# Neighbourhood operands, bias tables and two modulation groups made inside the pair attention, with the bias tables' masks on VectorE

## What is computed

```
x = first_block(x, c, ctx, c_ctx, norm_gain, w_mod, ...)   # DEPTH = 2 layers
return second_block(x, p_2, ...)

# one layer of the first block, cut
modulation of c by w_mod (six groups), norm, one projection to all operands
att  = global_gqa(q, k, v, k_ctx, v_ctx)       # 8 query heads, 2 key heads of 64, 1280 keys
pool = pool_branch(z, w, s)
near = neighbourhood_attn(q, k, v, k_ctx, v_ctx, rpb, rows)   # 4 heads, bias table by relative place
x = x + gate * (concat(att, pool, near) @ w_out)
```

## Time and profile before

| | us |
|---|---|
| median of 3 runs | 3750.84 |
| lowest and highest | 3748.06, 3755.4 |
| the profiled execution, its own time | 3751.04 |
| its span in the trace | 3749.3 |
| busy PE, DVE, POOL, ACT | 3528.4, 2018.6, 1842.0, 1209.2 |
| layer 0: operand stage starts, step 0's scores start | 388.9, 449.0 |
| layer 1: the same | 1270.8, 1312.3 |

### The profile page before, as it was taken

One profiled execution on the slowest core, in us unless ns is written; L12 is line 12 of the kernel. 1 busy time (PEld: TensorE's weight loads), 2 busy tenths in 40 slices (PEclk: granted clock), 3 DMA queues, 4 the chain that ended last, 5 costly groups with the idle time before them and its releaser, 6 DMA issues. The chain is left out here.

```text
span 3749.3 us, 54629 instructions
## 1 busy us (share of the span) xinstructions
PE 3528.4 (94%) x22582; PEld 2715.0 (72%) x22582; DVE 2018.6 (54%) x2278; ACT 1209.2 (32%) x1716; POOL 1842.0 (49%) x1028
## 2 busy tenths in 40 slices
PE   5999899889899899889999999989899999999998
PEld 5888644568788754568887777876587788878877
DVE  4443577552454467553566734555542888884142
ACT  3234244431223344431123422325401444441020
POOL 1443266544255266543455643304444699974433
PEclk9999899999999999999999999999999999999999
DMA  5112200025111200022221220020033122234212
GB/s 189 35 42 69 75 1 1 27 108 207 57 40 61 58 1 1 27 109 83 94 70 45 86 89 24 4 102 1 27 119 140 52 85 85 85 110 163 64 45 73
DMA packets 101933, 257.99 MB, mean 69 GB/s; under 512 B 29232, under 2 KB 38576, under 8 KB 100800
## 3 DMA queue, kind: packets, MB, share of 16 engines
q1 hardware_dynamic: 83008, 215.42, 16.6%
q10 hardware_dynamic: 18688, 39.20, 3.1%
HBM read 200.02 MB, written 54.56 MB: 68 GB/s over the span
## 5 line engine op out<-in xcount | busy, mean ns | idle before, releaser
L1876 PE MATMUL acc<-h_hi,weights_hi 128*128 128x512 f32 (+1 forms) x928 | 347.5, 374 | 6.6 <-DVE h_lo L2045 4.2
L1877 PE MATMUL acc<-h_lo,weights_hi 128*128 128x512 f32 (+1 forms) x928 | 339.0, 365 | 0.0
L1878 PE MATMUL acc<-h_hi,weights_lo 128*128 128x512 f32 (+1 forms) x928 | 338.7, 365 | 0.0
L1104 DVE TENSOR_REDUCE part_max<-aux 128x1 f32<-128x428 f32 (+5 forms) x468 | 252.9, 582 | 152.5 <-PE aux L945 109.8
L2583 PE MATMUL acc<-h_hi,weights_hi 128*128 128x512 f32 x672 | 271.4, 404 | 0.0
L2585 PE MATMUL acc<-h_hi,weights_lo 128*128 128x512 f32 x672 | 262.9, 391 | 0.0
L2584 PE MATMUL acc<-h_lo,weights_hi 128*128 128x512 f32 x672 | 262.3, 390 | 0.0
L2059 DVE RECIPROCAL arena<-arena 128x512 f32<-128x512 f32 (+1 forms) x48 | 141.8, 2953 | 223.2 <-ACT arena L2022 223.2
L1066 ACT ACTIVATE probs<-acc 128x1024 f32<-128x1024 f32 (+1 forms) x168 | 168.4, 1003 | 239.6 <-PE acc L980 236.8
L991 PE MATMUL acc<-probs,v_tok 128*64 128x512 f32 (+3 forms) x864 | 218.3, 585 | 2.5 <-DVE inverse L1124 2.5
L1876 PEld LDWEIGHTS acc<-h_hi,weights_hi 128*128 128x128 f32 x928 | 175.7, 189 | 41.2 <-issue 9.2
(11 more groups left out here) (524 smaller groups left out, 8976.3 us busy)
## 6 DMA issues: line engine op xcount, KB each, us to landing
weights<-in_w_in SPq DMA_DIRECT2D x44, 512.0 KB, 3.5
arena<-in_w_mod SPq DMA_DIRECT2D x6, 2048.0 KB, 9.3
weights<-in_w_up SPq DMA_DIRECT2D x24, 512.0 KB, 4.3
weights<-in_w_out SPq DMA_DIRECT2D x22, 512.0 KB, 4.9
weight_sums<-feed_forward_spill SPq DMA_DIRECT2D x22, 512.0 KB, 4.6
xT<-in_w_up SPq DMA_DIRECT2D x20, 512.0 KB, 4.1
weights<-in_w_mod SPq DMA_DIRECT2D x4, 2048.0 KB, 21.3
mixer_gates<-arena SPq DMA_DIRECT2D x32, 256.0 KB, 2.0
```

Source lines behind the costliest of these rows:

```text
L1104: nc.vector.tensor_reduce(part_max[:, b % 2, j, hh, i:i + 1], max_tile(m)[:, hh, 0:cw], AX_X, ALU.max, negate=True).then_inc(max_done, 1)
L1876: nc.tensor.matmul(out, w_hi[:, b, k, :], hi[:, k, cols], start=(k == 0), stop=False)
L1877: nc.tensor.matmul(out, w_hi[:, b, k, :], lo[:, k, cols], start=False, stop=False)
L1878: return nc.tensor.matmul(out, w_lo[:, b, k, :], hi[:, k, cols], start=False, stop=(k == KD - 1))
```

## The change

`attention_operands` and its block are gone. A class `AttentionOperands` holds the same work, cut into tasks, and `pair_attention` puts these into its own order, in both layers of the first block:

- Ahead of row 0 (`ahead`): turns 0 to 2, then 12 dense matmuls and the twelve maxima of block 0 with two dense ones ahead of each of the next four; flips 0 to 3 behind maxima 4, 6, 8 and 10, each waiting until ACT has copied the former one's bank to the table in SBUF (`keep_head`, 128x1024); in layer 0 the product of the first gate; row 0. ACT begins with one exponential of a single column (`warm`), then rounds the first key head and the first 512 queries; DVE rounds its halves of both.
- In the steps (`within`): turns 3 to 8 in half-steps 4 to 9, the second key head's rounding on ACT and its rest on DVE, in layer 0 the second gate. Of block 1's maxima, the four that had stood ahead of step 0 in layer 0, and all others, are spread evenly over the steps up to row 1.
- The bias tables: mask, add and copy with rim for each of four heads (`table_step`) on DVE, in half-steps from the fifth on that hold no maximum, `prep` or part of a reciprocal. All their operands are in SBUF. POOL has none of them (`BY_POOL = 0`).
- One slot for the gates' weights in place of two: SP loads the second when the first product is through.
- SP issues all diagonals; POOL clears two of their rows, sets the row of ones, makes the rest of the first key head and the fill.

```diff
@@ -843,10 +843,22 @@
                 at -= 1
             tasks.setdefault(at, []).insert(0, ("max", m))
         at -= 1
-        if first == first_exp[p]:
+        if first == first_exp[p] and (p or not early_in):
             for i in reversed(range(n_prep)):
                 tasks.setdefault(at - (n_prep - i), []).insert(0, ("prep", p, i))
+    if early_in:
+        taken = {at for at in tasks if any(task[0] in ("max", "invert", "prep") for task in tasks[at])}
+        for at, task in AttentionOperands.within(gated, taken):
+            tasks.setdefault(at, []).insert(0, task)
     order = [task for at in sorted(tasks) if at < 0 for task in tasks[at]]
+    if early_in:
+        order, later = AttentionOperands.ahead(gated, order)
+        end = next(at for at in tasks if ("row", 1) in tasks[at])
+        held = later + [task for at in range(end) for task in tasks.get(at, ()) if task[0] == "max"]
+        for at in range(end):
+            tasks[at] = [task for task in tasks.get(at, ()) if task[0] != "max"]
+        for i, task in enumerate(held):
+            tasks[1 + i * (end - 1) // len(held)].append(task)
...
@@ -1003,13 +1040,27 @@
 
                 for at, (kind, j, *i) in enumerate(order):
                     if kind == "max":
-                        if at < n_ahead:
+                        if early and at < n_ahead:
+                            if j < 5:
+                                keep_busy(pg, score_slots[0], first_idle if j == 0 else 2)
+                        elif at < n_ahead:
                             keep_busy(pg, outs[1], first_idle if j == 0 else 2 if pieces[j][0] == 0 else 4)
                         maximum(j)
                     elif kind == "row":
-                        if at < n_ahead:
+                        if early and at < n_ahead:
+                            pe.wait_ge(early.kept_flip, NA_HEADS)
+                            keep_busy(pg, score_slots[0], 5)
+                        elif at < n_ahead:
                             keep_busy(pg, outs[1], 5)
                         row(j)
+                    elif kind == "turn":
+                        early.turn(pe, j)
+                    elif kind == "flip":
+                        early.flip_head(pe, j)
+                    elif kind == "gate_product":
+                        early.gate_product(pe, j)
+                    elif kind == "gate_turn":
+                        early.gates.turn(pe, j)
                     elif kind == "sums":
                         sums(j)
                     elif kind == "scores":
...
@@ -1127,8 +1195,20 @@
                         out = pairs[p].q[:, q0:q0 + qn]
                         nc.vector.tensor_tensor(out, out, inverse[:, 0:qn], ALU.mult).then_inc(divided, 1)
 
+                if early:
+                    early.first_by_vector(dve, pairs[0].q, qs[:, 0], wide)
                 for kind, j, *i in order:
-                    if kind == "prep":
+                    if kind == "first_parts":
+                        early.low_by_vector(dve, pairs[0].q, qs[:, 0], slice(0, wide))
+                    elif kind == "rest_dve":
+                        early.rest_by_vector(dve, pairs[0].q, qs[:, 0], slice(wide, q_cols))
+                    elif kind == "second_rest":
+                        early.second_by_vector(dve)
+                    elif kind == "table":
+                        early.table_step(dve, j, *i)
+                    elif kind == "gate_add":
+                        early.gates.add(dve, j)
+                    elif kind == "prep":
                         if (j, i[0]) == (0, 0):
                             first_copies()
                         if i[0] in ((5, 7) if own_keys else (1, 3)):
...
+class AttentionOperands:
...
+    BY_POOL = 0
+
+    @staticmethod
+    def within(gates, taken):
+
+        found = [(4 + i, ("turn", 3 + i)) for i in range(6)]
+        found += [(2, ("second_keys", 0)), (4, ("second_keys", 1)), (6, ("second_rest", 0))]
+        if gates:
+            found += [(1, ("gate_add", 0)), (1, ("gate_turn", 0)), (2, ("gate_keep", 1)), (2, ("gate_product", 1)), (3, ("gate_add", 1)), (3, ("gate_turn", 1))]
+        steps = [("table", h, i) for h in range(AttentionOperands.BY_POOL, NA_HEADS) for i in range(3)]
+        free = [at for at in range(5, 150) if at not in taken]
+        return found + list(zip(free, steps))
+
+    @staticmethod
+    def ahead(gates, order):
+
+        row = order.index(("row", 0))
+        first, later = [("turn", 0), ("turn", 1), ("turn", 2), ("first_shift", 0), ("rest_act", 0)], order[row + 1:]
+        for kind, j, *i in order[:row]:
+            first.append((kind, j, *i))
+            if kind == "max" and j in (4, 6, 8, 10):
+                first.append(("flip", (j - 4) // 2))
+        if gates:
+            first += [("gate_product", 0), ("gate_keep", 0)]
+        return first + [("first_parts", 0), ("rest_dve", 0), ("row", 0)], later
+
...
+    def sync(self, sp):
+        I = self.pg.ins
+        for h in range(NA_HEADS):
+            sp.dma_start(self.diag[0:64, h, 0:15, :], self.diagonals(h)).then_inc(self.placed[h], 16)
+            sp.dma_start(self.diag[64:P, h, 1:16, :], self.diagonals(h)).then_inc(self.placed[h], 16)
+            if h == 0:
+                sp.dma_start(self.flip[:], I["c_flip"]).then_inc(self.masks_loaded, 16)
+                sp.dma_start(self.mask[:], I["c_colmask"]).then_inc(self.masks_loaded, 16)
+                if self.gates:
+                    self.gates.fetch(sp, 0)
+        if self.gates:
+            self.gates.fetch(sp, 1)
...
+    def turn(self, pe, g):
+        tiles, dst = self.groups[g]
+        bank = self.banks[g % 2 if g < 3 else 1]
+        if g == 3 and self.gates:
+            pe.wait_ge(self.gates.added, 2)
+        if g >= 2:
+            pe.wait_ge(self.copied, g - 1 if g < 4 else g)
+        for j, tile in enumerate(tiles):
+            mm = self.pg.nc.tensor.transpose(bank[:, j * P:(j + 1) * P], tile, self.cn["ident"][:])
+        mm.then_inc(self.turned, 1)
+
+    def flip_head(self, pe, h):
+        pe.wait_ge(self.placed[h], 32)
+        if h == 0:
+            pe.wait_ge(self.masks_loaded, 32)
+            pe.wait_ge(self.cleared, 2)
+        else:
+            pe.wait_ge(self.kept_flip, h)
+        for c in range(2):
+            mm = self.pg.nc.tensor.matmul(self.table_bank[:, c * BANK:(c + 1) * BANK], self.flip[:],
+                                          self.diag[:, h, c * 8:c * 8 + 8, :].rearrange("p a n -> p (a n)"), start=True, stop=True)
+        mm.then_inc(self.flipped, 1)
+
+    def gate_product(self, pe, i):
+        if i == 0:
+            pe.wait_ge(self.copied, 2)
+        else:
+            pe.wait_ge(self.gates.added, i)
+        self.gates.product(pe, i)
...
+    def keep(self, act, g):
+        tiles, dst = self.groups[g]
+        bank = self.banks[g % 2 if g < 3 else 1]
+        act.wait_ge(self.turned, g + 1)
+        self.pg.nc.scalar.copy(dst, bank[:, 0:len(tiles) * P].rearrange("p (a n) -> p a n", n=P)).then_inc(self.copied, 1)
+
+    def keep_head(self, act, h):
+        act.wait_ge(self.flipped, h + 1)
+        self.pg.nc.scalar.copy(self.table[:, h], self.table_bank.rearrange("p (a n) -> p a n", n=GRID_W)).then_inc(self.kept_flip, 1)
+
+    def second_by_scalar(self, act, half):
+        self.pg.nc.scalar.copy(self.k_twice[half * HD:(half + 1) * HD, 1, :], self.k[HD:P]).then_inc(self.second_made, 1)
...
+    def table_step(self, dve, h, i):
+        nc, table, inner = self.pg.nc, self.table[:, h], self.inner[:, h]
+        n = h - self.BY_POOL
+        if i == 0:
+            dve.wait_ge(self.kept_flip, h + 1)
+            dve.wait_ge(self.fill_made, 1)
+            nc.vector.tensor_tensor(table, table, self.across(self.mask), ALU.mult).then_inc(self.masked, 1)
+        elif i == 1:
+            dve.wait_ge(self.masked, n + 1)
+            nc.vector.tensor_tensor(table, table, self.across(self.fill), ALU.add).then_inc(self.filled, 1)
+        else:
+            dve.wait_ge(self.filled, n + 1)
+            nc.vector.tensor_copy(inner, self.table[:, h, 3:13]).then_inc(self.inner_made, 1)
+            dve.wait_ge(self.inner_made, 4 * n + 1)
+            nc.vector.memset(inner[0:64, 8:10], -NEG).then_inc(self.inner_made, 1)
+            nc.vector.memset(inner[64:P, 0:1], -NEG).then_inc(self.inner_made, 1)
+            nc.vector.memset(inner[64:P, 9:10], -NEG).then_inc(self.inner_made, 1)
...
@@ -2209,7 +2383,9 @@
                 blocks.append((SEQ, CTX, [(t, 0, False) for t in range(SEQ // P, n_tiles)]))
             return Pair(mix[:, p, 0:SEQ + q_ctx * P], maxima, blocks, lambda t, hh: v_tok[:, t, kv * HD:(kv + 1) * HD],
                         keys=(k_twice[:, kv, :], k_rest[:, kv, :]))
-        pair_attention(pg, cn, [query_pair(p) for p in range(4)], SEQ + q_ctx * P, [by_head(5), total[:]], 4, 12 if last else 4, by_head(4))
```

(21 more changed lines are left out.)

276 lines of the change are left out of this document (146 added, 130 removed).

## The result

The changed kernel takes 3765.11 us (median of 7 runs, 3763.44 to 3767.35) against 3753.19 for the one before (7 runs on the same chip): slower by 12 us, ratio 1.003, 95% interval 1.0020 to 1.0039. Forecast were 3759, and 8 us slower than the profiled execution of before.

A forecast was written before the change was run, and what follows sets the result against it. PE, busy 3528.4 of 3749.3 us, bounds the kernel through waits and its lower clock. Gain 20.2 up to row 1, less 2.8 in layer 0 and 20.9 + 4.6 in layer 1, gives -8.1: 3751.0 + 8.1 = 3759, range 3735 to 3770.

The forecast's parts named there:

- Way to step 0: From the operand stage's start to step 0's scores: shorter by 27.3 us in layer 0 and 9.7 in layer 1.
- Steps to row 1: First steps after step 0, now holding all twelve pieces, turns and second gate: loss 12.4 us in layer 0, 4.4 in layer 1.
- The wait for the gate's load: Step 1 of layer 0: PE waits 2.5 us for the second gate's 2 MB, with everything behind it.
- 18.4 for twelve pieces at 1.11 and 0.4: Layer 0, steps up to row 1: block 1's twelve pieces, 1.11 us of DVE and 0.4 of hand-over each, 18.4 us.
- Steps 18 and 38 of layer 1: Table steps alternating with POOL's additions delay the reduction: 7.2 us at each place, plus 4.6 for lower-clock work behind both.
- Steps 9, 29 and 49: Layer 1: a mask (9, 49) or copy (29) waits for POOL's turn; losses 2.4, 1.7 and 2.4 us.
- Layer 0 behind row 1: Later table steps in layer 0 lose 2.8 us together.
- Steps 27 and 28: Layer 0: add and copy of head 2, at step 27, exceed the idle time by 1.5 us.
- Sum: Gain 20.2 us up to row 1, less 2.8, 20.9 and 4.6: 8.1 us slower, 3759.
- copies are not free: Rival: copies run beside POOL's turn, steps 18 and 38 cost 4.4 us each, step 29 nothing; 3749 us, chance 0.15.
- DVE does not run through: Rival: DVE's next instruction takes its turn before POOL, so steps 18, 38 and 29 fit idle time; 3738 us, chance 0.26.
- The lower clock at the first flip: Rival: in one layer dense matmuls do not raise the clock, 0.5 at first flip; 10 us more, 3769 us, chance 0.19.

## Why the prediction was right, step by step

The direction, the mechanism and the sum held; single terms were off in both directions, and that the sum came so near is in part luck.

- *Way to step 0* (27.3 and 9.7): 30.7 and 12.4. The parts stand in the order forecast and the clock was at 1.00 at the first flip, which takes 1.98 us. The chain was some 3 us shorter than summed: turn 2 came 3.7 us behind the stage's start in place of 4.2, it and the dense matmuls took 4.5 us (394.13 to 398.60) in place of 5.7, since the clock rose among them, the five maxima 4.5 (398.60 to 403.13) in place of 5.5, and a flip comes every 3.15 us in place of 3.3, with ACT's copy at 1.01.
- *Steps to row 1* (12.4 and 4.4): 11.3 and 4.5. The wait for the gate's load was 1.05 us, not 2.5; step 2 nevertheless came 4.4 us later than its pace, with the product's 1.95 and DVE's and PE's waits behind it. (The prediction's 18.4 for twelve pieces at 1.11 and 0.4 is 18.1.) What the twelve pieces themselves cost here was not tested by a run.
- *Steps 18 and 38 of layer 1* (7.2 each and 4.6 for the clock, 19.0): 6.7 + 1.9 each, 17.3. The reduction started late by three turns of POOL between DVE's steps, 10.2 us behind the addition beside POOL where the sum had 11.3, and PE waited 6.11 us at the first of the two. That is the step on which the sign rested, and the run with one operand in place of two shows it: of the 24 us that masks and adds cost in steps 9 to 79, 2 are left.
- *Steps 9, 29 and 49* (2.4, 1.7, 2.4): 3.8, 3.7 and 3.8. The delays were sized well for two of them (2.4, 2.3, 2.4); what was left out is the clock. PE waits 2.05, 1.90 and 2.02 us there, the clock fell behind each, and that cost 1.4 us each time. The prediction had put a clock loss on the long waits alone.
- *Layer 0 behind row 1* (2.8): 7.8. Here a step was missed or far too small: the mask of head 3, behind step 31's scores, stands right behind a subtraction of the next pair's queries, like those of layer 1, takes 3.28 us and costs 4.1 us with its clock; it is not named in the list, which has no more than 0.5 for the steps that it does not name. Steps 27 and 28 cost 1.7 (1.5 forecast), steps 17 and 18 0.8 (0.4). The last 1.3 us, at step 56, are no table step: DVE and POOL alternate there before as after the earlier trace rows, and PE waits 2.0 us in both, but in the changed kernel the clock fell to 0.51.
- *Sum*: +8.1 forecast, +9.4 in the edited stretches. The two errors, 6 us too little gain and 7 us too little loss, nearly cancel, and that is luck. The rest of the measured 12 us lies within what single executions scatter outside; whether a small part of it belongs to the change was not settled.
- *Rivals*: copies are not free (the copy of step 29 alone costs 4.8 us in the run without masks and adds). DVE does not run through: the row of 2.75 and 3.25 us has POOL's turn in each. The lower clock at the first flip did not come.

## What to carry to other kernels

When work is moved off a serial stage into a pipeline, look at what it will stand beside: here 24 DVE instructions (8 masks, 8 adds, 8 copies) that cost 1.22 us or less alone cost up to 3.3 us each beside POOL's additions, and what counted was not DVE's load (54%) but that the next instruction in DVE's queue fed PE. The remedy was to give each instruction one operand in PSUM and to do it where the operand already lay there, ahead of step 0: of the 41 us gained at the front 24 were kept, and the kernel came to 3728 us against 3752 before. The two halves of the remedy were not tried apart in the steps: the masks from PSUM keep 1.22 us beside POOL's table adds, and ahead of step 0 POOL's additions of the sums have not begun. After a wait of PE, carry a term for the clock.
